# Three instead of four plain tile pairs at the head of each feed-forward stage, with VectorE splitting pieces five and six

## The reference

```python
def swiglu(x, w_gate, w_up, w_down):
    return (jax.nn.silu(x @ w_gate) * (x @ w_up)) @ w_down
...
    for l in range(DEPTH):
        h = layer_norm(a * h + 0.5 * swiglu(h, ffn1_w_gate[l], ffn1_w_up[l], ffn1_w_down[l]),
                       ln1_g[l], ln1_b[l])
        ...
        h = layer_norm(a * h + 0.5 * swiglu(h, ffn2_w_gate[l], ffn2_w_up[l], ffn2_w_down[l]),
                       ln3_g[l], ln3_b[l])
```

## Time and profile before

| | us |
|---|---|
| median of three runs | 1888.67 (1888.56 to 1888.8) |
| time of the profiled execution | 1891.47 |
| its span, first to last instruction | 1889.7 |

### The profile page before, as it was taken

How to read it: one execution, slowest core, us unless ns; L and a number is a source line. 1 busy time by engine, 2 the same in 40 slices (tenths; PEclk the granted TensorE clock), 3 DMA queues, 4 the chain that set the end, 5 groups by cost and what they waited for, 6 DMA issues and landing times.

```text
span 1889.7 us, 34669 instructions
## 1 busy us (share of the span) xinstructions
PE 1856.0 (98%) x14406; PEld 1774.5 (94%) x14406; DVE 1181.7 (63%) x1834; ACT 882.0 (47%) x1357; POOL 348.4 (18%) x200
## 2 busy tenths in 40 slices
PE   8999999999999999999999999999999999999997
PEld 8999999999899999999999999999997779899895
DVE  5728637568447827728487286476683478286475
ACT  4524525474336534525465254255742465255253
POOL 3030210410001140130420302104100120402113
PEclk9999999999998999999999999999999999999998
DMA  4323322556444332333533333225655543233232
GB/s 157 101 90 113 112 81 99 157 134 134 105 103 96 101 112 90 102 92 101 143 101 103 92 108 113 90 95 152 143 126 112 112 95 106 89 112 115 87 113 90
DMA packets 57469, 206.73 MB, mean 109 GB/s; under 512 B 6368, under 2 KB 6368, under 8 KB 57312
## 3 DMA queue, kind: packets, MB, share of 16 engines
q1 hardware_dynamic: 48240, 171.78, 29.1%
q0 software_dynamic: 8640, 31.46, 9.0%
q10 hardware_dynamic: 432, 1.25, 0.2%
HBM read 202.38 MB, written 2.10 MB: 108 GB/s over the span
## 4 chain that ended last, share of the span: by engine, by line
PE 96%; DVE 2%; ACT 1%; issue 0%; DMA 0%; ACTq 0%; DVEq 0%
PE PS L462 13%; PE PS L465 13%; PE PS L464 13%; PE PS L401 9%; PE PS L402 9%; PE PS L403 9%; PE PS L442 6%; PE PS L443 6%; PE PS L444 6%; PE PS L411 2%; PE PS L433 2%; PE PS L412 2%; PE PS L727 1%; PE PS L562 1%; PE PS L758 1%; DVE h_lo L1208 0%
## 5 line engine op out<-in xcount | busy, mean ns | idle before, releaser
L358 POOL TENSOR_TENSOR w_lo<-raw,w_hi 128x1024 fp32r<-128x1024 f32 x112 | 284.0, 2541 | 1083.7 <-ACT w_hi L916 1057.3
L401 PE MATMUL PS<-h_hi,w_hi 128*128 128x264 f32 (+1 forms) x1238 | 370.2, 299 | 0.5 <-DVE h_lo L1208 0.3
L402 PE MATMUL PS<-h_lo,w_hi 128*128 128x264 f32 (+1 forms) x1238 | 369.7, 299 | 0.0
L403 PE MATMUL PS<-h_hi,w_lo 128*128 128x264 f32 (+1 forms) x1238 | 369.4, 298 | 0.0
L916 ACT ACTIVATE w_hi<-raw 128x1024 fp32r<-128x1024 f32 x240 | 215.1, 930 | 233.0 <-PE PS L403 179.3
L462 PE MATMUL PS<-v_hi,s_hi 128*128 128x264 f32 (+1 forms) x864 | 244.8, 283 | 0.1
L464 PE MATMUL PS<-v_lo,s_hi 128*128 128x264 f32 (+1 forms) x864 | 244.3, 283 | 0.0
L465 PE MATMUL PS<-v_hi,s_lo 128*128 128x264 f32 (+1 forms) x864 | 243.9, 282 | 0.0
L401 PEld LDWEIGHTS PS<-h_hi,w_hi 128*128 128x128 f32 x1238 | 233.0, 188 | 9.2 <-DVE h_lo L1208 1.6
L402 PEld LDWEIGHTS PS<-h_lo,w_hi 128*128 128x128 f32 x1238 | 233.1, 188 | 7.4
L403 PEld LDWEIGHTS PS<-h_hi,w_lo 128*128 128x128 f32 x1238 | 232.3, 188 | 7.3
(11 more groups left out here) (226 smaller groups left out, 4112.4 us busy)
## 6 DMA issues: line engine op xcount, KB each, us to landing
raw<-in_stream SPq DMA_DIRECT2D x316, 512.0 KB, 3.7
w_lo<-in_stream POOLq DMA_DIRECT2D x60, 512.0 KB, 7.7
raw_first<-in_stream SPq DMA_DIRECT2D x4, 512.0 KB, 5.7
out_t<-X SPq DMA_DIRECT2D x8, 256.0 KB, 2.1
X<-in_x_t SPq DMA_DIRECT2D x7, 264.0 KB, 7.3
par<-in_params ACTq DMA_DIRECT2D x2, 480.0 KB, 3.4
X<-in_x_t ACTq DMA_DIRECT2D x1, 264.0 KB, 4.6
```

What stands on the lines that cost most here:

```text
L358: nc.gpsimd.tensor_tensor(w_lo[:, slot, :], raw[:, slot % RAWS, :], w_hi[:, slot, :].bitcast(F32), ALU.subtract).then_inc(lo_done[slot], 1)
L401: nc.tensor.matmul(o, hi, rhs_hi[:, k, tok], start=first, stop=False)
L402: nc.tensor.matmul(o, hi, rhs_lo[:, k, tok], start=False, stop=False)
L403: return nc.tensor.matmul(o, lo, rhs_hi[:, k, tok], start=False, stop=last)
```

## The change

`CLASSIC` goes from 4 to 3: tile 3 (pieces 6 and 7) becomes a seven-product pair in each of the four feed-forward blocks. The pieces left to split whole, 4 and 5, go from GpSimd to VectorE (`by_vector`). VectorE's list at the head is reordered; in particular the low part of raw piece 6 stands behind only one of the four sums, so SP has a second wait, for all four sums, before it overwrites that slot. The last plain tile's `h_hi` and `h_lo` move behind the first copy and behind the next sums.

```diff
-CLASSIC = 4
+CLASSIC = 3
...
+def fast_gates():
+    return {gate_piece(l, f, m) - 1: fast_index(l, f, m) for l in range(DEPTH) for f in range(2) for m in range(CLASSIC, MT)}
...
+def by_vector(n):
+    r = n % LAYER_PIECES
+    r -= 0 if r < FFN_PIECES else FFN_PIECES + MIX_IN + MIX_OUT
+    return SLOTS <= r < 2 * CLASSIC
@@ sync: the loop that loads raw pieces
                     wait_piece(sp, n - RAWS)
+                    if n - RAWS in pair_of:
+                        sp.wait_ge(S["s_sum_done"], 4 * pair_of[n - RAWS] + 4)
@@ gpsimd
-                elif whole(n):
+                elif whole(n) and not by_vector(n):
                     split(n)
@@ scalar, ffn
-                            h_high(m, m0, F22, span)
+                            if m < CLASSIC - 1:
+                                h_high(m, m0, F22, span)
...
                             .then_inc(S["p1_copied"], 1)
+                        if m == CLASSIC:
+                            h_high(m - 1, m0, F22, span)
@@ vector, ffn
                             if m == CLASSIC - 1:
-                                for j in range(1, 5):
+                                for j in range(2, 5):
                                     sum_low(fast_index(l, f, CLASSIC), j)
...
                             product_of(m, F22, span, 0.5)
-                            h_low(m, m0, F22, span)
+                            if m == 0:
+                                raw_low(FP + 4, slice(0, 2 * BLOCK))
+                            if m < CLASSIC - 1:
+                                h_low(m, m0, F22, span)
                             if m == 0:
                                 v_sums(l, f, span, (2, 4))
+                                raw_low(FP + 5, slice(0, 2 * BLOCK))
+                                v_low(l, f, span, 3)
                                 v_low(l, f, span, 1)
+                            elif m == 1:
                                 v_low(l, f, span, 2)
-                            elif m == 1:
-                                v_low(l, f, span, 3)
                                 v_low(l, f, span, 4)
                             if m == CLASSIC - 2:
-                                w_sums(fast_index(l, f, CLASSIC), gate + 4, S_ORDER)
-                                pair_low(gate + 4)
+                                w_sums(fast_index(l, f, CLASSIC), gate + 4, S_ORDER[0:1])
+                                raw_low(gate + 4, slice(0, 2 * BLOCK))
+                                sum_low(fast_index(l, f, CLASSIC), 1)
+                                w_sums(fast_index(l, f, CLASSIC), gate + 4, S_ORDER[1:4])
+                                raw_low(gate + 5, slice(BLOCK, 2 * BLOCK))
                             continue
...
                             w_sums(i + 1, gate + 2, S_ORDER)
+                        if m == CLASSIC:
+                            h_low(m - 1, m0, F22, span)
```

More of the change, by code:

```diff
@@ L324, in _ @@
         def _(sp):
+            pair_of = fast_gates()
             for kind, n in START_ORDER:
```

## The result

| | before | after |
|---|---|---|
| median of the runs on one chip, us | 1889.38 (1888.56 to 1890.76, six runs) | 1904.47 (1901.07 to 1907.95, six runs) |
| profiled execution, us | 1891.47 | 1901.07 |
| its span, us, and mean granted clock | 1889.7, 0.989 | 1899.3, 0.990 |

The ratio is 1.0078, with a 95% interval of 1.0064 to 1.0093: the changed kernel is slower by 0.78%, between 12.1 and 17.6 us. The same kernel in a later group of runs gave 1.0068 (1.0053 to 1.0083), between 10.0 and 15.7 us.

What follows compares the result with a forecast made beforehand. TensorE, busy 98% of the span, was taken to bound the kernel. Fewer matmuls -5.3, the fourth block's stall -0.5 and new waits +17.9 gave +12.0 us on 1888.67: 1900.7 us, range 1895 to 1909.

Steps and rivals of the forecast that it cites:

- The waits: First block, tile 3: piece 9 lands late, so the seven-product pair waits 4.37 us and the block is 2.93 us longer.
- The choice of 4.5 us for the load: Piece 9's load, issued soon after piece 8's, takes 4.5 us, between bounds of 3.6 (alone) and 4.6.
- The shares: Tile 3's 4.37 us wait splits over product three (some 0.7 us), five (another 1.4) and seven (remaining 2.2).
- The first share: Product three of tile 3 is some 0.7 us late, waiting for ScalarE's first copy behind three `s_hi` and a `silu`.
- The sum: Whole kernel: fewer matmuls -5.3, fourth block's old stall -0.5, new waits +17.9, together +12.0 us.
- matmuls go away: Each block loses 12 matmuls: 1.44 us each in blocks one to three, 1.01 in the fourth, 5.3 us together.
- tiles 4 and 5 had lost: Fourth block, kernel before: tile 4's pair loses 0.51 us waiting for VectorE's addition, and this loss goes away.
- the new waits: Waits in the seven-product pair of tile 3: 4.37 us in three blocks, 4.75 in the fourth, +17.9 us together.
- Tile 4: no wait: Tile 4's product seven, due at 70.11 in the first block, could start at 70.10: no wait, but no cover.
- VectorE's `v_lo` and `v_sum` are much shorter while GpSimd is silent: VectorE's head: each takes 1.17 us with GpSimd silent, against a 3.34 us `v_sum` and median 2.3 us `v_lo`.
- The rival on the clock: Waits ahead of product seven also cost clock, 1.7 us per stretch; one to four give 1902.4 to 1907.5 us; chance 0.20.

Runs made afterwards that it cites:

- the run with the splits alone: Kernel before with its four plain pairs, only the splits of pieces 4 and 5 moved from GpSimd to VectorE: 1889.69 us, ratio 0.9992.
- the reordered head: Changed kernel with one `v_sum` ahead of tile 0's `h_lo`, and tile 1's sums and both splits ahead of `v_lo` 4 and `s_lo` 1: 1890.52 us, ratio 0.9995.
- the kernel with early copies: Changed kernel with ScalarE's two copies of tile 3 ahead of the high parts of pieces 8 and 9: 1910.02 us, ratio 1.0100.
- the early addition: Changed kernel with VectorE's addition for product seven ahead of the `h_lo` and splits in tile 3 alone: 1907.87 us, ratio 1.0083.

## Why the prediction was right

It gave 1900.7 us, in a range from 1895 to 1909; the change costs 15.1 us at the medians, the forecast said 12.0.

**The waits.** In the first block each step came where it was put. Counted from the up piece of tile 1: piece 9 loaded at 19.71 (forecast 19.76), first sum at 24.17 (24.26), addition at 29.73 (29.85), product seven at 30.31 (30.44), tile 4 at 31.86 (31.94). The choice of 4.5 us for the load, near the row for a second load and not the 3.6 of a load alone, was the decisive one: it took 4.46. The prediction also worked out 3.2 us from the fit in "DMA: Bandwidth & Descriptors" of the Trainium skill (section "Anatomy of one DMA — SWDGE (gpsimd) path"). The page gives that fit for transfers that GpSimd issues, and this load is issued by SP, so it was the wrong one to take; it would have moved the sum the wrong way by about 5 us. The shares were 0.59, 1.20 and 2.19 us, where 0.7, 1.4 and 2.2 were forecast; the rest of the 4.29 us by which the pair is longer is 0.1 us in each product right behind a wait. The first share was put on ScalarE's copy, rightly, though the view names `s_lo` in the first block.

**The sum.** The four stages are 11.5 us longer in the first profile, against 12.0. In blocks one to three each is 2.80 to 2.87 us longer, forecast 2.93. In the fourth the terms are further off than their sum, 2.98 against 3.23. An undisturbed pair takes 9.82 us there, so 1.31 us of matmuls go away and not 1.01, and tiles 4 and 5 had lost 1.1 us before and not 0.51. On the other side the new waits are 5.4 us and not 4.75: 4.9 in tile 3, and 0.5 in tile 4, for which none was forecast. That 0.9 us one way and 0.7 us the other nearly cancel is luck. "Tile 4: no wait" held in blocks one to three.

**VectorE and GpSimd.** That VectorE's `v_lo` and `v_sum` are much shorter while GpSimd is silent held: `v_lo` took 1.21 us and occupied 1.17, as forecast. While GpSimd still split beside it, in the run with the splits alone, two `v_lo` took 4.63 us together, at the same place 2.42 after:

```profile
36.81 4.63 DVE L1250 TENSOR_TENSOR v_lo<-v_sum,v_hi 128x1056 fp32r<-128x1056 f32 x2
```

The Trainium skill ("SBUF — State Buffer", section "Who interferes with whom") describes one pair of ports that the two engines share and lock against each other; these rows agree.

**The rest, and the clock.** The change costs 15.1 us at the medians of the first group and 12.9 by the ratio of the second. The first profile's stages account for 11.5 us, which lies inside the interval of the second group (from 10.0) and just below that of the first (from 12.1). So a rest of up to a few microseconds is likely, and no term of the forecast's sum holds it. The rival on the clock, at 0.20, does, and was partly true. Executions of the changed kernel spread over 6.9 us with their mean clock: the one at 0.986 took 1907.95, those at 0.989 took 1904.1 to 1905.3, those at 0.990 1901.07 to 1903.68. At a mean clock of 0.990 the kernel before took 1891.1 on average (six runs) and the one after 1902.0 (four runs), 10.9 us apart, which is the stages' 11.5 to within a microsecond. At 0.989 the averages are 1891.3 (two runs) and 1904.9 (three), 13.6 us apart. The mean clock is given to 0.001, which is 1.9 us of such a time, so these comparisons can't be finer. The two profiles of the changed kernel lost the clock behind the new wait in one block of eight, at 1.1 us; the second profile's stages, with that loss and 0.45 us of other lateness, account for 13.05 us. The rival's cause is seen at work once, and its rate, one to four blocks in each execution, was too high by the two profiles. That the unprofiled, slower executions lost it in the same place is argued only, since they left no trace; the stretches at the lower level between the blocks also vary, at the norm behind the second block from 3.4 to 10.2 us over the ten profiles, and in the two of the changed kernel 10.2 and 6.8.

**What the runs tell of the cause.** VectorE's list at the head decides when piece 9 is loaded: one step more costs its time once a block (1.35 us), the same steps in another order give the added 2.8 to 3.0 us back, and moving the addition alone only moves the wait to tile 4. The added wait of SP was not tried away, since the load would then overwrite a slot that the sums still read. What it costs is not shown. It holds piece 8 back until just before piece 9, and two loads close together are slower than one, 4.6 against 3.6 us in the earlier trace rows. But in the reordered head it is met before it is asked for, the two loads still start 0.6 us apart, and the time is back; so the change doesn't need that wait gone.

## What to carry to other kernels

When a stage of cheaper arithmetic is begun one tile earlier, look first at what it needs to have loaded, and count back along the engine that frees the buffer: matmuls saved come to nothing while a slot is freed late, and here three microseconds in each block were won back by putting the steps that free a slot ahead of those that don't. If an engine's wait disappears when one step is moved, see whether it stands one tile further on. Where a wait of TensorE can't be removed, look at how it is cut: here 4 to 5 us in three or four pieces between matmuls mostly kept the clock, and much the same time with one piece of 2.5 us or more lost it each time. And when a view names a releaser, see whether it is the instruction that the program's semaphore asks for.

## What the runs showed of the hardware

One uninterrupted wait of 3.2 to 4.2 us was followed by the lower clock level (a granted clock of 0.51, 1.2 GHz) for 3.4 or 6.8 us in eight blocks of eight, in the two profiles of the kernel with early copies, and so were those of 2.5 to 3.2 us in the four blocks with the early addition. About the same time of waiting in three pieces, of 0.6, 1.2 and 2.2 us with matmuls between them, was followed by it in one block of eight (1.0, 1.3 and 2.2 us in the fourth block), and four pieces of 0.6 to 2.2 us in none of four. The early copies left the total wait of TensorE as it was, and the kernel became some 5 us slower (1910.0 against 1904.7 us in the same group). The Trainium skill ("TensorE: Matmul & The Clock Gate", Part 1) says that the slow level is the default and sustained activity releases it, and these rows agree. In them the longest piece of a wait goes with the loss of the level, and not only the sum of the pieces. Why one block of eight lost it with a longest piece of 2.2 us, and the others with the same pieces did not, stays open.

While GpSimd subtracted beside it, VectorE's 128 x 1056 `v_lo` took 2.3 us, and 1.21 us while GpSimd was silent (4.63 and 2.42 us for two). In the kernel after, the matmul that waited for VectorE's addition started 0.15 us behind its end in all four blocks, and the one that waited for ScalarE's copy 0.05 us behind.
